# Gated DeltaNet layer: no products with the zero state of a head's first chunk, no update of the state behind its last chunk

## The chip, the cores and the metric

One NeuronCore of a Trainium2 chip runs the whole program. The metric is the device time of one execution in microseconds (us); the kernel before took 1097.52 us in the median of three runs (1096.98 to 1097.6).

## The reference

The sizes are batch 1, 1024 tokens, width 1024 and a depth of one layer, so of the three mixers only the gated DeltaNet runs. It is adaLN modulation (shift, scale and gate from `c`) and RMS norm, one input projection, the mixer, an output projection, a gated residual add and a final RMS norm. The mixer has 8 heads with keys of 128 and values of 256 numbers. Queries, keys and values pass through a causal convolution of four taps and SiLU; queries and keys are normalised. Per head a state S of 128x256 starts at zero, and with a chunk's solved matrices u, w, its attention a and its decayed queries and keys the scan does

```python
def step(S, inp):
    q_c, a_c, u_c, w_c, k_c, gl_c = inp
    v_new = u_c - w_c @ S
    o_c = q_c @ S + a_c @ v_new
    S = S * gl_c + k_c.T @ v_new
    return S, o_c
```

so in the first chunk of a head both products with S are zero, and the S that the last chunk makes is not read. The output is normalised, multiplied by SiLU(z) and projected. All is float32.

## The kernel before

The work is cut into 16 units: unit u = 2*head + par is half `par` (512 tokens) of a head, in 4 chunks of 128 tokens (the kernel's chunks are longer than the reference's; the result is the same). Unit 0 stands ahead of a loop, the loop over `hd` has 7 iterations of two units (an odd one, then an even one), and unit 15 stands behind it. Each engine has its own program, written out by hand, and engines meet by semaphores that only count up; `passed(engine, name, u, n)` waits until maker `name` has counted to n in unit u.

TensorE's program for a unit (`body`) has three kinds of work. One is the input projection of the next unit: six tiles of 24 matmuls each (`project`, L449), a float32 product as three products of high and low parts. It is cut into pieces that stand between the other steps (`fill`; FILLS gives their lengths): by the end of the three merge steps and the piece behind `turn_v` tiles 0, 1 and 2 are done, and tile 3 begins in chunk 0. The second kind is the chunk's matrix inverse (`merge_p`, `merge_d`), and the third the recurrence, per chunk c: K·S (L597), Q·S (L601), a piece of projection, X = inverse · rhs (L609), a piece, the state's increment (L619), the attention's product (L622), a piece, and from chunk 2 on the output projection of chunk c-2 (L567).

Each of these products has a partner elsewhere. VectorE makes the right-hand side `r_rhs` from K·S and the scaled values `vt` (L1232), updates `state` (L1255, after a memset at L1217 in even units) and adds the output's two parts (L1261). ScalarE scales Q·S (`scale_q`, L837) and X (`scale_x`, L843). Semaphores `ks_done`, `qs_done`, `r_done`, `x_done`, `x_out`, `kv_done`, `av_done`, `state_done` and `o_done` count these, four a unit (`state_done` five).

Weight tiles reach TensorE in four steps with two buffers: a DMA of 512 KB issued by SP's queue in a fixed order (`load_tile`, L289), the high part by ScalarE (`split_hi`, L745), the low part by GpSimd (`split_lo`, L1479), the matmuls. The output projection's weights come by the same buffers once per head (`load_wo`, L304), are multiplied by the gate on VectorE (L1111) and split (L751, L1486). For the inverse VectorE makes the matrix of the next unit (`make_n`, L1088), SP takes it through a buffer in HBM into blocks of 16 (L308, L310), VectorE inverts the blocks step by step, SP brings them back (L314, L316), and VectorE spreads them (L1124) for the first merge of the next unit (L513).

Of the kernel before, what the change touches and what calls it, by code (L numbers as in the profile page):

```python
# [7 lines left out]
ALU = mybir.AluOpType  # L8
ACT = mybir.ActivationFunctionType

P = 128
# [4 lines left out]
DV = 256  # L16
# [7 lines left out]
NCH = HALF // P  # L24
# [15 lines left out]
def build(nc, x, c, ada_w, ada_b, norm_w, w_in, conv_w, a_log, dt_bias, gdn_norm_w, w_out,  # L40
          final_norm_w, out):
    ctx = ExitStack()
    with ctx:
# [49 lines left out]
        state = sb("state", [P, DV])  # L93
# [5 lines left out]
        cvk = part(0, 1024, to="p (s t) -> p s t", s=2)  # L99
        cvq = part(1024, 1024, to="p (s t) -> p s t", s=2)  # L100
# [7 lines left out]
        vt = part(5120, 1024, to="p (c t) -> p c t", c=NCH)  # L108
# [324 lines left out]
        def _(pe):  # L433
# [138 lines left out]
            def body(hd, par, last=False, begun=0, fills=FILLS):  # L572
                u = 2 * hd + par
                pos = [begun]
                in_merge, in_v, in_chunk, in_tail = fills

                def fill(n):
                    n = min(n, 2 * MM - pos[0]) if last else n
                    project(u, par, pos[0], pos[0] + n, last)
                    pos[0] += n  # L580

                for lv in range(3):
                    merge_p(u, lv)
                    if lv == 2 and not last:
                        turn_k(u + 1, 1 - par)
                        k_gram(u + 1, 1 - par)
                    fill(in_merge[lv][0])
                    merge_d(u, lv)
                    fill(in_merge[lv][1])
                turn_v(u)  # L590
                fill(in_v)

                for c in range(NCH):
                    passed(pe, "state_done", u, c + 1)
                    if c == 0:
                        passed(pe, "v_scaled", u, 4)
                    nc.tensor.matmul(bank[2][:, 0:DV], cvk[:, par, c * P:(c + 1) * P], state[:, :],  # L597
                                     start=True, stop=True).then_inc(S["ks_done"], 1)
                    passed(pe, "og_done", u, max(c - 1, 0))
                    passed(pe, "qs_scaled", u, c)  # L600
                    nc.tensor.matmul(bank[3][:, 0:DV], cvq[:, par, c * P:(c + 1) * P], state[:, :],  # L601
                                     start=True, stop=True).then_inc(S["qs_done"], 1)
                    if c >= 2:
                        out_project(u, c - 2, 0, hd, par, not last)
                    fill(in_chunk[c][0])
                    if c == 0:
                        passed(pe, "u_merged", u, 3)
                    passed(pe, "r_done", u, c + 1)
                    nc.tensor.matmul(bank[4][:, 0:DV], u_fin[:, c, :], r_rhs, start=True, stop=True  # L609
                                     ).then_inc(S["x_done"], 1)  # L610
                    if c >= 2:
                        out_project(u, c - 2, 1, hd, par, not last)
                    fill(in_chunk[c][1])
                    if c > 0:
                        turn_o(u, c - 1)
                    passed(pe, "x_out", u, c + 1)
                    if c == 0:
                        passed(pe, "kdec_done", u, 1)
                    nc.tensor.matmul(bank[4][:, DV:2 * DV], kdec[:, par, c, :], xs, start=True, stop=True  # L619
                                     ).then_inc(S["kv_done"], 1)  # L620
                    passed(pe, "o_done", u, c)
                    nc.tensor.matmul(bank[5][:, 0:DV], attn_t[:, c, :], xs, start=True, stop=True  # L622
                                     ).then_inc(S["av_done"], 1)
                    fill(in_chunk[c][2])
                fill(in_tail)
                turn_o(u, NCH - 1)
                for n in range(2):
                    out_project(u, NCH - 2, n, hd, par, not last)
                if not last:
                    qk(u + 1, 1 - par)  # L630
                    turn_q(u + 1, 1 - par)
                for n in range(2):
                    out_project(u, NCH - 1, n, hd, par, not last)
# [104 lines left out]
        def _(act):  # L738
# [95 lines left out]
            def scale_q(u, c):  # L834
                passed(act, "qs_done", u, c + 1)
                passed(act, "o_done", u, c)
                nc.scalar.activation(qss, bank[3][:, 0:DV], ACT.Identity, scale=e_gc[:, u, c:c + 1]  # L837
                                     ).then_inc(S["qs_scaled"], 1)
# [24 lines left out]
            def body(hd, par, last=False, first=False):  # L863
# [32 lines left out]
                if not last:  # L896
                    split_hi(u, hd, par, 3)
                for c in range(NCH):
                    scale_q(u, c)
                    if not last:  # L900
                        if c == 0:
                            evacuate_z(u, 2, 1)
                        elif c == 1:
                            evacuate(u, par, hd + par, 3)
                    scale_x(u, par, c)
                    if c > 0:
                        og_high(u, c - 1, last)
# [106 lines left out]
        def _(dve):  # L1014
# [136 lines left out]
            def merge_d_out(u, lv):  # L1151
# [17 lines left out]
                else:  # L1169
                    u_odd = u_fin[0:64, :, 64:P]  # L1170
                    nc.vector.tensor_tensor(u_odd, u_odd, bank[4][0:64, 0:DV].rearrange("p (c w) -> p c w", c=NCH),
                                            ALU.subtract).then_inc(S["u_merged"], 1)

            def norm_y(t):
                if t == 0:
                    dve.wait_ge(fw_in, 16)
                dve.wait_ge(fin_pow, t + 1)
                for j in range(0, D_MODEL, D_MODEL if t < TILES - 1 else HALF):
                    cols = slice(j, D_MODEL if t < TILES - 1 else j + HALF)
                    stt(out=y[:, t, cols], in0=y[:, t, cols], scalar=frs[:, t:t + 1], in1=w_raw[:, 0, cols],  # L1180
                        op0=ALU.mult, op1=ALU.mult).then_inc(fin_done, 1)
# [7 lines left out]
            def body(hd, par, last=False, first=False):  # L1189
# [22 lines left out]
                merge_p_out(u, 2)  # L1212
                if not last:
                    sum_g(u + 1)
                if par == 0:
                    passed(dve, "qs_done", u, 0)
                    nc.vector.memset(state[:, :], 0.0).then_inc(S["state_done"], 1)  # L1217
                else:
                    dve.sem_inc(S["state_done"], 1)
                merge_d_out(u, 2)  # L1220
                if last:
                    silu(u, 0, zt[:, 0, :], gate=True)
# [3 lines left out]
                    make_n(u + 1, other)  # L1226

                for c in range(NCH):
                    passed(dve, "ks_done", u, c + 1)
                    passed(dve, "v_scaled", u, c + 1)  # L1230
                    passed(dve, "x_done", u, c)
                    stt(out=r_rhs, in0=bank[2][:, 0:DV], scalar=neg_egc[:, u, c:c + 1], in1=vt[:, c, :],  # L1232
                        op0=ALU.mult, op1=ALU.add).then_inc(S["r_done"], 1)
                    if c == 0:
                        if last:
                            norm_y(1)
# [13 lines left out]
                            invert_blocks(u + 1, *BASE_STEPS[par][c])  # L1250
                    if c > 0:
                        gate_o(u, c - 1)
                    passed(dve, "kv_done", u, c + 1)
                    passed(dve, "qs_done", u, c + 1)
                    stt(out=state[:, :], in0=state[:, :], scalar=e_gl[:, u, c:c + 1], in1=bank[4][:, DV:2 * DV],  # L1255
                        op0=ALU.mult, op1=ALU.add).then_inc(S["state_done"], 1)
                    passed(dve, "av_done", u, c + 1)
                    passed(dve, "qs_scaled", u, c + 1)
                    passed(dve, "o_turned", u, c - 1)
                    passed(dve, "o_squared", u, c - 1)  # L1260
                    nc.vector.tensor_tensor(o_raw[:, c % 2, :], bank[5][:, 0:DV], qss, ALU.add  # L1261
                                            ).then_inc(S["o_done"], 1)
                    if last and c == 3:
                        gate_o(u, 3)
                    if c >= 2:
# [341 lines left out]
```

## Time and profile before

| | us |
|---|---|
| median of three runs | 1097.52 |
| the profiled execution | 1097.52 |
| its span, first to last instruction | 1095.5 |
| TensorE busy (matmuls) | 1033.7 |
| VectorE busy | 813.2 |
| ScalarE busy | 511.3 |
| GpSimd busy | 498.1 |

An engine's busy time is the time in which at least one of its instructions ran. A float32 product with 256 columns stands in the trace as two matmuls, so 64 products on a line are 128 records. Matmuls overlap: a record's duration is longer than the distance to the next record's start. "Idle before" in square brackets is the time in which the engine did nothing ahead of the instruction, with what ended it. The granted clock is 1.00 at 2.4 GHz and 0.50 at 1.2 GHz.

### The profile page before, as it was taken

To read this page: it belongs to the slowest core of one execution; us is meant where nothing else is said; L and a number is where in the kernel's file an instruction comes from. 1 tells how busy PE (TensorE), PEld (TensorE's weight loads), DVE (VectorE), ACT (ScalarE), POOL (GpSimd) and SP (SyncE) were. 2 spreads that over 40 slices of the span, in tenths; PEclk is the share of its full clock that TensorE was granted. 3 is DMA by queue.
4 is the path that set the end of the run, shared out by engine and by line. 5 is a ranking of instruction groups with operands and counts; after the bars stand their busy time and mean duration, and the time that the engine had idled before them with its cause. 6 is when DMAs were issued, how large, how long until landed. Compare 5 with 4: busy or idle time off the path is not lost.

```text
span 1095.5 us, 20950 instructions
## 1 busy us (share of the span) xinstructions
PE 1033.7 (94%) x6367; PEld 832.0 (76%) x6367; DVE 813.2 (74%) x1757; ACT 511.3 (47%) x1263; POOL 498.1 (45%) x722
## 2 busy tenths in 40 slices
PE   3898699999999999999999999999999999999996
PEld 3766487878778787878878787888878787887864
DVE  4779577697767787597867877686867967687866
ACT  3663444435344543545443543545344453545443
POOL 2242453446444652555435552546435453446424
PEclk9898899999999999999999999999999999999999
DMA  9922222223122221224222231213212241213212
GB/s 316 326 94 79 63 68 64 75 71 88 52 69 70 77 68 51 75 63 107 51 57 59 80 88 51 69 50 102 75 50 59 68 107 51 68 51 86 61 58 115
DMA packets 144440, 91.29 MB, mean 83 GB/s; under 512 B 21526, under 2 KB 136952, under 8 KB 144376
## 3 DMA queue, kind: packets, MB, share of 16 engines
q1 hardware_dynamic: 144376, 90.65, 29.6%
q14 instruction: 50, 0.41, 0.1%
q8 instruction: 14, 0.23, 0.1%
HBM read 81.69 MB, written 8.95 MB: 83 GB/s over the span
## 4 chain that ended last, share of the span: by engine, by line
PE 84%; DVE 5%; issue 5%; ACT 2%; DMA 2%; POOL 2%; SPq 1%; DVEq 0%; POOLq 0%; ACTq 0%
PE bank L449 44%; PE bank L567 17%; PE bank L609 3%; PE bank L597 3%; PE bank L601 2%; PE bank L619 2%; PE bank L622 2%; DVE y L1054 2%; PE bank L647 2%; PE bank L548 1%; PE bank L500 1%; PE bank L474 1%; DMA y<-in_x 1%; PE bank L520 1%; PE bank L539 1%
## 5 line engine op out<-in xcount | busy, mean ns | idle before, releaser
L1479 POOL TENSOR_TENSOR w_lo<-w_raw,w_hi 128x256 fp32r<-128x256 f32 x384 | 309.3, 836 | 277.3 <-ACT w_hi L745 277.3
L449 PE MATMUL bank<-h_hi,w_hi 128*128 128x512 f32 x760 | 328.5, 432 | 6.2 <-ACT w_hi L745 6.2
L449 PE MATMUL bank<-h_lo,w_hi 128*128 128x512 f32 x760 | 299.9, 395 | 0.0
L449 PE MATMUL bank<-h_hi,w_lo 128*128 128x512 f32 x760 | 204.1, 400 | 0.0
L449 PEld LDWEIGHTS bank<-h_hi,w_hi 128*128 128x128 f32 x760 | 143.7, 189 | 38.3 <-ACT w_hi L745 6.9
L1029 DVE SCALAR_TENSOR_TENSOR work<-pre,cw,work 128x512 f32<-128x512 f32 x192 | 160.8, 838 | 12.3 <-ACT work L772 4.2
L449 PEld LDWEIGHTS bank<-h_hi,w_lo 128*128 128x128 f32 x760 | 142.7, 188 | 29.8
L449 PEld LDWEIGHTS bank<-h_lo,w_hi 128*128 128x128 f32 x760 | 144.1, 190 | 26.9 <-issue 0.5
L1521 POOL TENSOR_TENSOR og_lo<-work,og_hi 128x256 fp32r<-128x256 f32 x62 | 45.7, 737 | 211.2 <-ACT og_hi L832 211.2
L567 PE MATMUL bank<-wo_hi,og_hi 128*128 128x512 f32 x248 | 110.1, 444 | 4.1 <-DVE y L1054 4.0
L1054 DVE SCALAR_TENSOR_TENSOR y<-bank,o_rs,y 128x512 f32<-128x512 f32 x128 | 89.8, 743 | 20.9 <-PE bank L567 20.3
L745 ACT ACTIVATE w_hi<-w_raw 128x1024 fp32r<-128x1024 f32 x96 | 101.6, 1058 | 2.1 <-DMA w_raw<-in_gdn_w_in 2.1
L567 PE MATMUL bank<-wo_hi,og_lo 128*128 128x512 f32 x248 | 97.5, 393 | 0.0
L567 PE MATMUL bank<-wo_lo,og_hi 128*128 128x512 f32 x248 | 97.4, 393 | 0.0
L786 ACT ACTIVATE work<-work 128x512 f32<-128x512 f32 x64 | 40.3, 629 | 108.2 <-DVE work L1029 108.2
L1232 DVE SCALAR_TENSOR_TENSOR work<-bank,neg_egc,work 128x256 f32<-128x256 f32 x64 | 30.8, 482 | 78.3 <-PE bank L597 77.5
L1103 DVE TENSOR_TENSOR work<-work 32x15 f32<-32x15 f32 (+7 forms) x240 | 76.8, 320 | 9.7 <-DVE work L1107 1.9
L1036 DVE SCALAR_TENSOR_TENSOR work<-work 128x512 f32<-128x512 f32 x96 | 73.6, 767 | 12.1 <-issue 10.2
L832 ACT ACTIVATE og_hi<-work 128x256 fp32r<-128x256 f32 x62 | 25.9, 418 | 115.8 <-DVE work L1045 107.4
L1486 POOL TENSOR_TENSOR wo_lo<-w_raw,wo_hi 128x256 fp32r<-128x256 f32 x64 | 56.9, 918 | 45.5 <-ACT wo_hi L751 45.5
L1045 DVE SCALAR_TENSOR_TENSOR work<-bank,small,work 128x128 f32<-128x128 f32 x128 | 38.9, 345 | 42.0 <-PE bank L548 41.8
L1107 DVE TENSOR_TENSOR work<-work 32x15 f32<-32x15 f32 (+7 forms) x240 | 62.4, 260 | 8.3
(196 smaller groups left out, 1663.7 us busy)
## 6 DMA issues: line engine op xcount, KB each, us to landing
w_raw<-in_gdn_w_in SPq DMA_DIRECT2D x96, 512.0 KB, 4.0
work<-in_ada_w SPq DMA_DIRECT2D x8, 1024.0 KB, 9.6
w_raw<-in_gdn_w_out SPq DMA_DIRECT2D x16, 512.0 KB, 4.4
y<-in_x SPq DMA_DIRECT2D x8, 512.0 KB, 9.0
work<-in_ada_w SPq DMA_DIRECT2D x8, 512.0 KB, 6.0
n_dram<-work SPq DMA_DIRECT2D x16, 256.0 KB, 2.3
work<-g_dram SPq DMA_DIRECT2D x15, 256.0 KB, 3.9
out<-y SPq DMA_DIRECT2D x7, 512.0 KB, 2.6
```

What stands on the lines that cost most here:

```text
L449: mm = nc.tensor.matmul(bank[m % 2][:, :], w[:, m % 2, k, :], h[:, k, half, :], start=(r == 0), stop=(r == MM - 1))
L567: mm = nc.tensor.matmul(out_bank(c, n, last)[:, :], a[:, m, :], w[:, m, n * 512:(n + 1) * 512], start=(m == 0 and q == 0), stop=(m == 1 an ...
L745: nc.scalar.activation(w_hi[:, k % 2, :, :], w_raw_k[:, k % 2, :, :], ACT.Copy).then_inc(S["w_hi_done"], 1)
L786: nc.scalar.activation(th[:, m % 2, :], cv, ACT.Tanh, scale=0.5).then_inc(S["tanh_done"], 1)
L1029: stt(out=cv, in0=pre[:, r, j:j + HALF], scalar=tap, in1=cv, op0=ALU.mult, op1=ALU.add).then_inc(S["conv_step"], 1)
L1036: stt(out=t, in0=th[:, m % 2, :], scalar=1.0, in1=t, op0=ALU.add, op1=ALU.mult).then_inc(S["silu_done"], 1)
L1054: i = stt(out=yt, in0=out_bank(c, n, last)[:, :], scalar=o_rs[:, c:c + 1], in1=yt, op0=ALU.mult, op1=ALU.add)
L1103: nc.vector.tensor_tensor(tmp, blk_n[:, j:j + 1, j + 1:].rearrange("p o n -> p n o").to_broadcast(shape), blk_y[:, j:j + 1, 0:j + 1].to_br ...
L1107: nc.vector.tensor_tensor(below, below, tmp, ALU.subtract).then_inc(S["base_step"], 1)
L1479: i = nc.gpsimd.tensor_tensor(w_lo[:, k % 2, j:j + 2, :], w_raw_k[:, k % 2, j:j + 2, :], w_hi[:, k % 2, j:j + 2, :].bitcast(F32), ALU.subt ...
L1486: o = nc.gpsimd.tensor_tensor(wo_lo[:, i, j:j + 256], w_raw[:, i, j:j + 256], wo_hi[:, i, j:j + 256].bitcast(F32), ALU.subtract)
L1521: nc.gpsimd.tensor_tensor(gated_lo(c, last), og, gated_hi(c, last).bitcast(F32), ALU.subtract).then_inc(S["og_lo_done"], 1)
```

## The change

TensorE's program: in chunk 0 of an even unit (`fresh`) the products K·S and Q·S go; two semaphore increments stand in their place, behind the same wait for the scaled values, and X takes the scaled values `vt` as its right side in place of `r_rhs`. In chunk 3 of an odd unit the increment of the state goes, with a semaphore increment in its place. ScalarE: the scaling of Q·S in a fresh chunk becomes an increment. VectorE: the memset of the state goes, the right-hand side of a fresh chunk becomes an increment, the state of a fresh chunk is a copy of the product, the last chunk's update becomes an increment, and the output of a fresh chunk is a copy in place of a sum.

```diff
                 for c in range(NCH):
-                    passed(pe, "state_done", u, c + 1)
-                    if c == 0:
+                    fresh = par == 0 and c == 0
+                    if fresh:
                         passed(pe, "v_scaled", u, 4)
-                    nc.tensor.matmul(bank[2][:, 0:DV], cvk[:, par, c * P:(c + 1) * P], state[:, :],
-                                     start=True, stop=True).then_inc(S["ks_done"], 1)
-                    passed(pe, "og_done", u, max(c - 1, 0))
-                    passed(pe, "qs_scaled", u, c)
-                    nc.tensor.matmul(bank[3][:, 0:DV], cvq[:, par, c * P:(c + 1) * P], state[:, :],
-                                     start=True, stop=True).then_inc(S["qs_done"], 1)
+                        pe.sem_inc(S["ks_done"], 1)
+                        pe.sem_inc(S["qs_done"], 1)
+                    else:
...
-                    passed(pe, "r_done", u, c + 1)
-                    nc.tensor.matmul(bank[4][:, 0:DV], u_fin[:, c, :], r_rhs, start=True, stop=True
+                    if not fresh:
+                        passed(pe, "r_done", u, c + 1)
+                    nc.tensor.matmul(bank[4][:, 0:DV], u_fin[:, c, :], vt[:, 0, :] if fresh else r_rhs, start=True, stop=True
                                      ).then_inc(S["x_done"], 1)
...
-                    nc.tensor.matmul(bank[4][:, DV:2 * DV], kdec[:, par, c, :], xs, start=True, stop=True
-                                     ).then_inc(S["kv_done"], 1)
+                    if par == 1 and c == NCH - 1:
+                        pe.sem_inc(S["kv_done"], 1)
+                    else:
...
                 for c in range(NCH):
-                    scale_q(u, c)
+                    if par == 0 and c == 0:
+                        act.sem_inc(S["qs_scaled"], 1)
+                    else:
+                        scale_q(u, c)
...
+            def update_state(u, par, c):
+                passed(dve, "kv_done", u, c + 1)
+                if par == 0 and c == 0:
+                    passed(dve, "qs_done", u, 0)
+                    i = nc.vector.tensor_copy(state[:, :], bank[4][:, DV:2 * DV])
+                else:
+                    passed(dve, "qs_done", u, c + 1)
+                    i = stt(out=state[:, :], in0=state[:, :], scalar=e_gl[:, u, c:c + 1], in1=bank[4][:, DV:2 * DV],
+                            op0=ALU.mult, op1=ALU.add)
+                i.then_inc(S["state_done"], 1)
...
-                if par == 0:
-                    passed(dve, "qs_done", u, 0)
-                    nc.vector.memset(state[:, :], 0.0).then_inc(S["state_done"], 1)
-                else:
-                    dve.sem_inc(S["state_done"], 1)
+                dve.sem_inc(S["state_done"], 1)
...
+                    if par == 0 and c == 0:
+                        dve.sem_inc(S["r_done"], 1)
+                    else:
...
+                    if par == 1 and c == NCH - 1:
+                        dve.sem_inc(S["state_done"], 1)
+                    else:
+                        update_state(u, par, c)
...
+                    if par == 0 and c == 0:
+                        nc.vector.tensor_copy(o_raw[:, c % 2, :], bank[5][:, 0:DV]).then_inc(S["o_done"], 1)
+                    else:
```

## Rows read from the trace of the kernel before

**Rows 1.** The page's busy line: busy us (share of span) and instructions:
```profile
PE 1033.7 (94%) x6367; PEld 832.0 (76%) x6367; DVE 813.2 (74%) x1757; ACT 511.3 (47%) x1263; POOL 498.1 (45%) x722
```

**Rows 2.** Busy by stretch: length, PE, PEld, DVE, ACT, POOL, granted clock, DMA:
```profile
235.00:1040.00 805.00, 795.84 (x4964) 643.52 (x4964) 609.78 (x1354) 374.32 (x948) 390.39 (x549) 1.00 0.27 69
```

**Rows 3.** Timeline of TensorE, unit 4, chunk 0: start us, duration us, line, operation:
```profile
382.57 0.60 PE L597 MATMUL bank<-state,work 128*128 128x256 f32 x2
...
383.25 0.58 PE L449 MATMUL bank<-h_hi,w_hi 128*128 128x512 f32 x1
...
383.66 0.40 PE L449 MATMUL bank<-h_lo,w_hi 128*128 128x512 f32 x1
...
384.13 0.39 PE L449 MATMUL bank<-h_lo,w_hi 128*128 128x512 f32 x1
```

**Rows 4.** Timeline of TensorE, unit 3, chunk 3:
```profile
348.18 0.60 PE L619 MATMUL bank<-work 128*128 128x256 f32 x2
348.62 0.59 PE L622 MATMUL bank<-work 128*128 128x256 f32 x2
```

**Rows 5.** Timeline of ScalarE and TensorE at tile 3, unit 2, then unit 4:
```profile
256.84 1.06 ACT L745 ACTIVATE w_hi<-w_raw 128x1024 fp32r<-128x1024 f32 x1 [0.84 <-DMA w_raw<-in_gdn_w_in]
...
258.29 0.58 PE L449 MATMUL bank<-h_hi,w_hi 128*128 128x512 f32 x1
...
381.06 1.06 ACT L745 ACTIVATE w_hi<-w_raw 128x1024 fp32r<-128x1024 f32 x1 [0.24 <-DMA w_raw<-in_gdn_w_in]
```

**Rows 6.** Timeline of TensorE and ScalarE, unit 0, chunk 0:
```profile
132.49 0.67 PE L597 MATMUL bank<-state,work 128*128 128x256 f32 x2 [1.75 <-ACT work L826]
...
134.47 0.50 PE L449 MATMUL bank<-h_hi,w_hi 128*128 128x512 f32 x1 [0.88 <-ACT w_hi L745]
...
133.36 1.06 ACT L745 ACTIVATE w_hi<-w_raw 128x1024 fp32r<-128x1024 f32 x1 [1.02 <-DMA w_raw<-in_gdn_w_in]
```

**Rows 7.** Timeline of VectorE and TensorE at the ends of units 1 and 3:
```profile
232.32 1.23 DVE L1111 TENSOR_TENSOR w_raw<-w_raw,gate_bc 128x1024 f32<-128x1024 f32 x1 [0.69 <-DMA w_raw<-in_gdn_w_out]
...
234.06 0.68 DVE L1124 TENSOR_TENSOR work<-work,diag_mask 128x512 f32<-128x512 f32 x1
...
234.89 0.44 PE L513 MATMUL bank<-work 128*32 128x16 f32 x32
...
358.50 0.68 DVE L1124 TENSOR_TENSOR work<-work,diag_mask 128x512 f32<-128x512 f32 x1
...
359.89 0.45 PE L513 MATMUL bank<-work 128*32 128x16 f32 x32
```

**Rows 8.** Timeline of GpSimd and TensorE, end of unit 15:
```profile
1080.43 0.73 POOL L1521 TENSOR_TENSOR og_lo<-work,og_hi 128x256 fp32r<-128x256 f32 x1 [4.03 <-ACT og_hi L832]
...
1081.21 0.50 PE L567 MATMUL bank<-wo_hi,og_hi 128*128 128x512 f32 x1
```

**Rows 9.** L212 on TensorE's sequencer: count, duration ns min/median/max, first, last start:
```profile
L212 PEldq EVENT_SEMAPHORE  x15: 51/51/51, 0.9 to 3.0; - x15
```

**Rows 10.** Timeline of VectorE and TensorE, unit 4, chunks 0 and 1:
```profile
388.30 0.48 DVE L1255 SCALAR_TENSOR_TENSOR state<-state,e_gl,bank 128x256 f32<-128x256 f32 x1 [1.25 <-PE bank L619]
...
389.81 0.59 PE L597 MATMUL bank<-state,work 128*128 128x256 f32 x2
```

**Rows 11.** TensorE alone by stretch: stretch, length, busy (records), granted clock, DMA:
```profile
128.76:137.00 8.24, 5.61 (x32) 1.00 0.52 139
...
88.82:92.40 3.58, 0.00 (x2) 0.83 0.38 115
...
91.21:98.04 6.83, 5.64 (x13) 0.50 0.20 49
...
57.08:60.49 3.41, 3.31 (x8) 0.50 0.87 282
```

**Rows 12.** Chain of waits, then timeline of TensorE, at the loop's top:
```profile
298.20 1.73 issue
...
304.79 0.45 PE L517 MATMUL bank<-work 128*32 128x32 f32 x16 [0.65 <-DVE work L1165]
```

More of the change, by code:

```diff
@@ L593, in body @@
                 for c in range(NCH):
-                    passed(pe, "state_done", u, c + 1)
-                    if c == 0:
+                    fresh = par == 0 and c == 0
+                    if fresh:
                         passed(pe, "v_scaled", u, 4)
-                    nc.tensor.matmul(bank[2][:, 0:DV], cvk[:, par, c * P:(c + 1) * P], state[:, :],
-                                     start=True, stop=True).then_inc(S["ks_done"], 1)
-                    passed(pe, "og_done", u, max(c - 1, 0))
-                    passed(pe, "qs_scaled", u, c)
-                    nc.tensor.matmul(bank[3][:, 0:DV], cvq[:, par, c * P:(c + 1) * P], state[:, :],
-                                     start=True, stop=True).then_inc(S["qs_done"], 1)
+                        pe.sem_inc(S["ks_done"], 1)
+                        pe.sem_inc(S["qs_done"], 1)
+                    else:
+                        passed(pe, "state_done", u, c + 1)
+                        if c == 0:
+                            passed(pe, "v_scaled", u, 4)
+                        nc.tensor.matmul(bank[2][:, 0:DV], cvk[:, par, c * P:(c + 1) * P], state[:, :],
+                                         start=True, stop=True).then_inc(S["ks_done"], 1)
+                        passed(pe, "og_done", u, max(c - 1, 0))
+                        passed(pe, "qs_scaled", u, c)
+                        nc.tensor.matmul(bank[3][:, 0:DV], cvq[:, par, c * P:(c + 1) * P], state[:, :],
+                                         start=True, stop=True).then_inc(S["qs_done"], 1)
                     if c >= 2:
@@ L618, in body @@
                         passed(pe, "kdec_done", u, 1)
-                    nc.tensor.matmul(bank[4][:, DV:2 * DV], kdec[:, par, c, :], xs, start=True, stop=True
-                                     ).then_inc(S["kv_done"], 1)
+                    if par == 1 and c == NCH - 1:
+                        pe.sem_inc(S["kv_done"], 1)
+                    else:
+                        nc.tensor.matmul(bank[4][:, DV:2 * DV], kdec[:, par, c, :], xs, start=True, stop=True
+                                         ).then_inc(S["kv_done"], 1)
                     passed(pe, "o_done", u, c)
@@ L1228, in body @@
                 for c in range(NCH):
[L1229 to L1233, printed above, removed]
+                    if par == 0 and c == 0:
+                        dve.sem_inc(S["r_done"], 1)
+                    else:
+                        passed(dve, "ks_done", u, c + 1)
+                        passed(dve, "v_scaled", u, c + 1)
+                        passed(dve, "x_done", u, c)
+                        stt(out=r_rhs, in0=bank[2][:, 0:DV], scalar=neg_egc[:, u, c:c + 1], in1=vt[:, c, :],
+                            op0=ALU.mult, op1=ALU.add).then_inc(S["r_done"], 1)
                     if c == 0:
@@ L1252, in body @@
                         gate_o(u, c - 1)
[L1253 to L1256, printed above, removed]
+                    if par == 1 and c == NCH - 1:
+                        dve.sem_inc(S["state_done"], 1)
+                    else:
+                        update_state(u, par, c)
                     passed(dve, "av_done", u, c + 1)
@@ L1260, in body @@
                     passed(dve, "o_squared", u, c - 1)
-                    nc.vector.tensor_tensor(o_raw[:, c % 2, :], bank[5][:, 0:DV], qss, ALU.add
-                                            ).then_inc(S["o_done"], 1)
+                    if par == 0 and c == 0:
+                        nc.vector.tensor_copy(o_raw[:, c % 2, :], bank[5][:, 0:DV]).then_inc(S["o_done"], 1)
+                    else:
+                        nc.vector.tensor_tensor(o_raw[:, c % 2, :], bank[5][:, 0:DV], qss, ALU.add
+                                                ).then_inc(S["o_done"], 1)
                     if last and c == 3:
```

## The prediction

> **What bounds the kernel now.** I first read the busy line of the page. TensorE is busy 1033.7 us of the span, 94% [rows 1]. Then I asked for one long stretch of the loop over heads, from 235 to 1040 us: TensorE is busy 795.84 of 805.00 us, 99%, at the full granted clock, with VectorE at 609.78 [rows 2]. So in the loop TensorE has 9.2 us without work, and an instruction taken from it shortens the loop, as long as nobody it waits for has become the last one. The question is therefore twofold: what one of the removed products takes of TensorE's stream, and at which of the places the stream can't close up because a tile, a DMA or another engine arrives only then.
>
> I call a head's first half unit 2*head and its second half unit 2*head+1. Each of the 8 heads loses two products (L597, L601) in chunk 0 of its even unit and one (L619) in chunk 3 of its odd unit, 24 of the 256 products on L597, L601, L619 and L622.
>
> **What a product takes.** In unit 4 the first state product starts at 382.57 and the second projection matmul behind the pair at 383.66, 1.09 us later; the projection matmuls of the tile follow each other in 0.23 us (two distances from 383.66 to 384.13) [rows 3]. Without the pair the first projection matmul stands where the first product stood, and the second comes 0.23 us later. So a pair is worth 1.09 - 0.23 = 0.86 us, 0.43 a product. The product behind the last chunk agrees: it starts at 348.18 and the next at 348.62 [rows 4], 0.43 to 0.44 us. If all 24 closed up it would be 24 x 0.43 = 10.3 us. Now place by place.
>
> **Pairs of units 4 to 14.** What is late next is the weight tile behind the pair (tile 3), split by ScalarE on L745. In unit 4 that split starts at 381.06 and takes 1.06, so it ends at 382.12; its first matmul starts at 383.25 [rows 3, 5]: 1.13 us in hand. The matmul of head 0 that does wait for such a split starts 0.05 us after it (133.36 + 1.06 = 134.42, then 134.47) [rows 6], so 1.08 us can be taken out and 0.86 is. I take unit 4 for all six (units 4, 6, 8, 10, 12, 14): 6 x 0.86 = 5.2 us.
>
> **Pair of unit 2.** Here the same split waited 0.84 us for its DMA, ends at 256.84 + 1.06 = 257.90, and the matmul starts at 258.29 [rows 5]. Only 0.39 - 0.05 = 0.34 us can go, and the remaining 0.52 becomes a wait for ScalarE.
>
> **Pair of unit 0.** TensorE sat idle 1.75 us before the pair, and then again 0.88 us until a tile 3 whose split waited 1.02 us for a DMA [rows 6]. Nothing removed here brings that DMA forward: 0 us. The same place has a price, below.
>
> **Products behind the last chunk.** In units 3, 5, 7, 9, 11 and 13 the stream goes on with the next product and with projections. The DVE chain at the unit's end (add y, gate the output weights, attention, spread) starts from TensorE's own results and moves with it. The merge that opens the next unit (L513) starts at 359.89, the spread it waits for ends at 358.50 + 0.68 = 359.18 [rows 7], 0.71 us earlier: covered for 0.43. If the DMA of the output weights landed only just in time there, these six would give nothing; I see no wait for it in unit 3 and take 6 x 0.43 = 2.6 us. In unit 1 there is such a wait: the gating on L1111 sat idle 0.69 us for that DMA, the spread ends at 234.06 + 0.68 = 234.74, and L513 starts at 234.89 [rows 7]. 0.15 - 0.05 = 0.10 us can go. In unit 15 the matmul of 1081.21 starts just behind GpSimd's split of 1080.43 + 0.73 = 1081.16 [rows 8], and that chain comes from a transpose ahead of the removed product: 0 us.
>
> Sum of what closes up: 5.2 + 0.34 + 2.6 + 0.10 = 8.2 us.
>
> **The rest of the edit.** 24 increments replace the products on TensorE. The 15 increments of the start take 51 ns each on its sequencer [rows 9]; the queue ahead of them hides that (0.05 x 24 = 1.2 us if it didn't, all in a row). I take 0. A copy of the state replaces memset and the fused update: the update of unit 4 took 0.48 us, ended at 388.78, and the next state product starts at 389.81 [rows 10], so it has 1.03 us in hand; a copy that is slower by that much would still cost nothing. VectorE no longer waits for the first state product and can make the next unit's matrix earlier, so its DMAs through n_dram start earlier, on a queue (SP's) that then comes to the next weight tile earlier; nobody on the path waits for them today: 0. On ScalarE one scaling per head goes, beside the idle time that the projections cover: 0.
>
> **The price in head 0.** With the pair gone TensorE does nothing from 132.49 - 1.75 = 130.74 to 134.47 us [rows 6], 3.73 us in one piece instead of 1.75 and 0.88. Before, it kept the full clock across these two gaps (1.00 over 128.76 to 137.00). An idle stretch of 3.58 us earlier (88.82 to 92.40) shows 0.83 as the granted clock, so it fell inside it, and the next 6.83 us ran at 0.50 with TensorE busy 5.64 of them; another half-clock stretch, 57.08 to 60.49, held 3.31 us of work [rows 11]. At half the clock (1.2 of 2.4 GHz) half of that time is lost: 1.7 us by the short one, 2.8 us by the long one. The new gap is 0.15 us longer than the one that brought the long one, but which of the two follows depends on when in the gap the clock falls, so I take the middle, 2.2 us; both ends stay in the range, and below them 0 for no fall. The Trainium skill (TensorE: Matmul & The Clock Gate, "Why this matters for your kernels") says that idle gaps between bursts of matmuls bring the lower clock back; by that rule the fall comes, and the case without one, below, would go.
>
> **Sum.** The profiled execution took 1097.52 us for a span of 1095.5, 2.0 around it, and is the median itself. 8.2 - 2.2 = 6.0 us off gives 1091.5 us.
>
> **Rivals.**
> *The clock doesn't fall in head 0.* Then the whole 8.2 us stay: 1089.3. For it: the two gaps now there were taken without a fall [rows 6, 11]. Against it: the 3.58 us gap.
> *The wait takes the product's place in all heads.* If the tile 3 of every even unit comes as late as in unit 2, the seven pairs give 7 x 0.34 = 2.4 instead of 5.5 us, and with 2.7 for the last chunks and the clock's 2.2 it comes to 1094.6. For it: two of the first three even units show a split that waits for its DMA. Against it: in unit 4 1.08 us are in hand.
> *An increment drains TensorE.* If it waited for the matmuls before it, each of the 14 places would cost about the difference between a matmul's duration and its distance to the next, 0.40 - 0.23 = 0.17 [rows 3], and a weight load, 832.0 us for 6367 of them or 0.13 [rows 1]: 14 x 0.30 = 4.2 us, which leaves 1095.7, no change that can be told. For it: the increments of before ran while the engine had nothing to do [rows 9]. Against it: the sequencer's waits stand before every tile and every state product, and the stream does not open there [rows 3].
> *The loop's top, on the other side.* At the top of the loop's second iteration the chain of waits runs through 1.73 us of issue time between two instructions of VectorE, and TensorE then waits 0.65 us on L517 for VectorE's transpose; the loop has seven iterations [rows 12]. VectorE's program gets another length ahead of the loop and inside it. If that puts one more such stop ahead of the transpose, each iteration loses 1.73, 7 x 1.73 = 12.1 us, and the time is 1103.6. It decides from 6.0 / 7 = 0.86 us an iteration on. For it: the stops are there, and nothing else explains them. Against it: few instructions change, so a stop may as well fall away.
>
> **Chances.** The forecast 0.55; no fall 0.2; the wait in all heads 0.1; the drain 0.07; the loop's top 0.05; the remaining 0.03 for something else that takes the gain. The predicted time is 1091.5. The range takes in no fall (1089.3), with some 1 us less at the loop's top, and the wait in all heads (1094.6): 1088.0 to 1095.0. What a measurement can tell from no change is 0.2%, 2.2 us, so "faster" is below 1095.3: the first three and part of the last, 0.87; "same" is the drain and a little of the rest, 0.08; slower 0.05.
>
> **What would show it.** L597 and L601 should have 56 products each instead of 64, L619 also 56, and TensorE's busy time in the loop should fall by about as much as the span. From unit 4 on, an even unit's first tile-3 matmul should follow the last matmul of tile 2 in 0.23 us. In unit 2 that matmul should wait about 0.5 us for L745. In head 0 TensorE should show one gap of some 3.7 us and a granted clock of half behind it. The L513 of unit 2 should wait for the spread. I am wrong if TensorE shows new idle time behind the increments, if the matmuls of other even units wait for L745, if the waits at the loop's top grow, or if the clock stays up in head 0.

## The result, and the profile after

The changed kernel took 1088.07 us (median of 4 runs, 1087.1 to 1089.54) against 1097.56 us for the kernel before beside it: ratio 0.9905, 95% interval 0.9888 to 0.9922. So 0.95% came off, some 9.5 to 10.4 us, where 6.0 was forecast; the time lies at or just below the low end of the forecast's range. The span of the profiled execution went from 1095.5 to 1086.9 us, 8.6 less; the sums below go by these spans (the profiled execution of after, 1088.6 us, is 0.5 slower than its median). (One run of an experiment, of the kernel with a filled gap and 8 increments, took 1702.8 us at a clock of 0.56; it is in none of the ratios below.)

Page of after, busy line, which answers to [rows 1]:

```profile
PE 1024.2 (94%) x6319; PEld 824.1 (76%) x6319; DVE 801.7 (74%) x1733; ACT 507.8 (47%) x1255; POOL 499.7 (46%) x722
```

TensorE has 48 records fewer (two for a product) and lost 9.5 us of work. To see the loop alone I take busy time by stretch from the L513 of unit 2 to the L513 of unit 15 (columns as in [rows 2]); after, then before:

```profile
237.71:1037.03 799.32, 792.54 (x4953) 640.19 (x4953) 604.06 (x1340) 375.15 (x955) 393.46 (x550) 1.00 0.27 70
```
```profile
234.89:1045.66 810.77, 801.34 (x4993) 647.82 (x4993) 613.74 (x1360) 378.54 (x962) 391.12 (x550) 1.00 0.26 69
```

The stretch is 11.45 us shorter, and TensorE's busy time in it fell by only 8.80: idle time went from 9.43 to 6.78. The removed products explain the first number, something else gave 2.65 us more, and 11.45 is more than the span lost because head 0, ahead of the loop, became longer. To place this, I cut the timelines of TensorE at two marks that every unit has, the start of its merge (L513, the first of unit u) and its first and last product with the inverse (X, L609 before, L616 after), and sum over units. Microseconds:

| kernel | even units 2 to 14: L513 to X of chunk 0 | odd units 3 to 13: L513 to X of chunk 0 | odd units 1 to 13: X of chunk 3 to next L513 | start of unit 1's L513 | span |
|---|---|---|---|---|---|
| before | 177.84 | 159.31 | 99.71 | 172.81 | 1095.5 |
| after | 171.46 | 156.70 | 96.91 | 175.85 | 1086.9 |
| e1: 1 increment | 171.50 | 158.33 | 96.54 | 174.15 | 1086.4 |
| e2: gap filled | 171.44 | 156.38 | 96.49 | 174.27 | 1084.5 |
| e3: pairs alone | 171.46 | 156.36 | 99.50 | 172.39 | 1085.6 |
| e4: last chunks alone | 177.83 | 158.86 | 96.85 | 173.64 | 1093.0 |
| e5: before, 31 increments | 177.81 | 154.23 | 99.69 | 174.96 | 1094.2 |
| e6: filled, 4 increments | 171.44 | 160.08 | 96.56 | 174.62 | 1088.6 |
| e7: filled, 8 | 171.44 | 154.50 | 96.53 | 174.14 | 1082.5 |
| e8: filled, 12 | 171.44 | 154.62 | 96.52 | 174.26 | 1083.3 |
| e9: 8 increments | 171.50 | 154.76 | 96.64 | 174.96 | 1083.7 |
| e10: after once more | 171.53 | 156.62 | 96.72 | 177.61 | 1088.3 |
| e11: e7 once more | 171.47 | 154.24 | 96.49 | 173.19 | 1081.3 |

The first column holds the removed pairs (unit 0 lies in the fourth), the second the loop's top in its six later iterations, the third the products behind a last chunk, the fourth head 0. After against before: -6.4, -2.6, -2.8, +3.0, together -8.7, and the span says -8.6. No odd unit lost a product in front of its first X, so the 2.6 us of the second column are the part that the forecast did not have.

Timeline of TensorE and ScalarE after, against [rows 3 to 5 and 7]: unit 2's L513 and its tile 3, the end of unit 3, tile 3 of unit 4:

```profile
237.71 0.45 PE L513 MATMUL bank<-work 128*32 128x16 f32 x32 [0.33 <-DVE work L1137]
...
258.66 1.10 ACT L755 ACTIVATE w_hi<-w_raw 128x1024 fp32r<-128x1024 f32 x1
...
260.43 0.39 PE L449 MATMUL bank<-h_hi,w_hi 128*128 128x512 f32 x1
...
349.42 0.60 PE L632 MATMUL bank<-work 128*128 128x256 f32 x2
349.67 0.58 PE L449 MATMUL bank<-h_hi,w_hi 128*128 128x512 f32 x1
...
381.56 1.98 PE L449 MATMUL bank<-h_hi,w_lo 128*128 128x512 f32 x8
383.37 0.39 PE L449 MATMUL bank<-h_hi,w_hi 128*128 128x512 f32 x1
383.60 0.39 PE L449 MATMUL bank<-h_lo,w_hi 128*128 128x512 f32 x1
```

In unit 4 the stream runs through the place of the pair in steps of 0.23 us with no gap: the increments there do not drain the engine. In unit 2 the split of tile 3 waits for nothing and ends at 258.66 + 1.10 = 259.76, 0.67 us ahead of its matmul.

Head 0, in the timeline of TensorE and by stretch (all engines), against [rows 6, 11]:

```profile
134.69 0.80 PE L449 MATMUL bank<-h_hi,w_hi 128*128 128x512 f32 x1 [4.46 <-ACT w_hi L755]
```
```profile
131.00:134.69 3.69, 0.00 (x0) 0.00 (x0) 1.76 (x8) 2.13 (x5) 0.00 (x0) 0.91 1.07 289
134.00:140.83 6.83, 6.14 (x14) 4.81 (x15) 0.00 (x0) 3.03 (x5) 2.79 (x4) 0.50 0.56 140
```

One idle piece of 4.46 us, where 3.73 was foretold, and from 134.00 on 6.83 us at half the clock (1.2 GHz), with 6.14 us of work in them. From that matmul to the L513 of unit 1 it is 41.16 us, against 38.34 before (134.47 [rows 6] to 172.81): the half clock costs 2.82 us. The other 0.22 of the 3.0 us is tile 3 itself, which starts later.

The loop's top, timeline of VectorE at the loop's second iteration, before and after:

```profile
300.06 0.42 DVE L1148 TENSOR_TENSOR pm<-bank,pair_mask 128x256 f32<-128x256 f32 x1 [1.86 <-issue]
300.40 0.16 DVE L1186 TENSOR_SCALAR q_eps<-q_ss 128x4 f32<-128x4 f32 x1
302.30 0.69 DVE L1036 SCALAR_TENSOR_TENSOR work<-work 128x512 f32<-128x512 f32 x1 [1.74 <-issue]
302.91 0.75 DVE L1029 SCALAR_TENSOR_TENSOR work<-pre,cw,work 128x512 f32<-128x512 f32 x1
```
```profile
301.76 0.43 DVE L1161 TENSOR_TENSOR pm<-bank,pair_mask 128x256 f32<-128x256 f32 x1 [1.65 <-issue]
302.10 0.20 DVE L1210 TENSOR_SCALAR q_eps<-q_ss 128x4 f32<-128x4 f32 x1
302.22 0.68 DVE L1049 SCALAR_TENSOR_TENSOR work<-work 128x512 f32<-128x512 f32 x1
304.19 0.75 DVE L1042 SCALAR_TENSOR_TENSOR work<-pre,cw,work 128x512 f32<-128x512 f32 x1 [1.29 <-issue]
```

VectorE stops twice in an iteration without waiting for any engine. Before, the second stop stood ahead of the SiLU product (L1036); after, that product (L1049) runs and the stop stands one instruction later, ahead of the convolution (L1042). The work of both is the same. The waits (total us, times, longest us) add it up over six iterations (the loop's first iteration has neither stop), before and then after:

```profile
DVE pm L1148 <- issue: 10.5, 6, 1.9
DVE work L1036 <- issue: 10.2, 6, 1.8
...
PE bank L517 <- DVE work L1165: 4.8, 8, 0.7
```
```profile
DVE pm L1161 <- issue: 10.0, 6, 1.9
DVE work L1042 <- issue: 8.1, 6, 1.5
...
PE bank L517 <- DVE work L1178: 2.7, 8, 0.8
```

The second stop costs 2.1 us less, and TensorE waits 2.1 us less for the transpose behind it. Two theories for that. A: the stop belongs to a position in VectorE's program; the change takes one instruction net from what VectorE runs ahead of the loop (312 records before, 311 after, waits and increments among them, register operations left out), so the same position falls one instruction later in the loop. B: VectorE simply has less to do (no fused update behind a last chunk, a copy for another). Beside these stands C, for head 0: the half clock comes from the idle piece that the pair left.

### The profile page after: what moved, and what is told of

Read it like the earlier page. It is cut to its first block, busy times and chain, and to the rows that moved or that the text cites. A ratio compares the mean times of both kernels' runs of the same rounds, so it can differ in the third digit from the quotient of the medians.

```text
span 1086.9 us, 20802 instructions
## 1 busy us (share of the span) xinstructions
PE 1024.2 (94%) x6319; PEld 824.1 (76%) x6319; DVE 801.7 (74%) x1733; ACT 507.8 (47%) x1255; POOL 499.7 (46%) x722
## 4 chain that ended last, share of the span: by engine, by line
PE 81%; DVE 7%; issue 4%; DMA 3%; ACT 2%; POOL 2%; SPq 1%; DVEq 0%; POOLq 0%; ACTq 0%
PE bank L449 43%; PE bank L567 16%; PE bank L616 3%; PE bank L632 2%; PE bank L603 2%; PE bank L607 2%; PE bank L629 2%; DVE y L1067 2%; PE bank L657 2%; PE bank L548 1%; PE bank L500 1%; PE bank L474 1%; DVE work L1042 1%; DMA w_raw<-in_gdn_w_out 1%; DMA y<-in_x 1%
## 5 line engine op out<-in xcount | busy, mean ns | idle before, releaser
L1505 POOL TENSOR_TENSOR w_lo<-w_raw,w_hi 128x256 fp32r<-128x256 f32 x384 | 305.4, 826 | 270.0 <-ACT w_hi L755 270.0
L1042 DVE SCALAR_TENSOR_TENSOR work<-pre,cw,work 128x512 f32<-128x512 f32 x192 | 161.0, 839 | 19.6 <-issue 8.1
L1049 DVE SCALAR_TENSOR_TENSOR work<-work 128x512 f32<-128x512 f32 x96 | 71.4, 744 | 13.9 <-ACT work L791 12.2
L853 ACT ACTIVATE work<-bank,k_tab 128x256 f32<-128x256 f32 x64 | 30.3, 474 | 76.3 <-PE bank L616 76.3
```

Source lines behind the costliest of these rows:

```text
L1042: stt(out=cv, in0=pre[:, r, j:j + HALF], scalar=tap, in1=cv, op0=ALU.mult, op1=ALU.add).then_inc(S["conv_step"], 1)
L1049: stt(out=t, in0=th[:, m % 2, :], scalar=1.0, in1=t, op0=ALU.add, op1=ALU.mult).then_inc(S["silu_done"], 1)
L1505: i = nc.gpsimd.tensor_tensor(w_lo[:, k % 2, j:j + 2, :], w_raw_k[:, k % 2, j:j + 2, :], w_hi[:, k % 2, j:j + 2, :].bitcast(F32), ALU.subt ...
```

## Experiments

**First set: e1 to e4**, beside the kernel before (median 1096.7 us of 13 runs).

e1 gives the missing position back: one increment of a semaphore that nobody waits for, on VectorE ahead of head 0.

```diff
+        pad = sem("pad")
...
+            for _ in range(1):
+                dve.sem_inc(pad, 1)
             body(0, 0, first=True)
```

> The changed kernel with one more semaphore increment in VectorE's program, on a semaphore nobody waits for, just ahead of unit 0. Theory A (the stop at the loop's top is tied to a position in VectorE's program, and the edit made that program one instruction shorter ahead of the loop): the stop comes one instruction earlier again, ahead of the SiLU of the unit's start instead of behind it, TensorE's waits for L517 and L532 go back from 4.4 us in all to about 7, and the span grows by 2 to 3 us against the changed kernel. Rival B (VectorE simply has less to do since the change): one increment of 21 ns changes nothing, the waits stay at 4.4 us and the span within 0.5 us, apart from the clock in head 0.

Its waits:

```profile
DVE work L1050 <- issue: 9.9, 6, 1.8
DVE pm L1162 <- issue: 9.6, 6, 1.7
...
PE bank L518 <- DVE work L1179: 4.8, 8, 0.8
```

L1050 is the SiLU product: the stop is back ahead of it, TensorE's wait is the 4.8 us of before, and the loop's top lost 1.6 of its 2.6 us, with every product still removed. That is A. The 1.0 us that stay are not the second stop's. Most of them go with the first: TensorE's wait on L532 behind it is 2.1 us in all before, 1.7 in after and 1.3 in e1, as that stop takes 10.5, 10.0 and 9.6; why it varies is open. The time does not show the loss: 1088.8 us, ratio 0.9928 (0.9912 to 0.9945), an interval that overlaps the changed kernel's, and instead of the 2 to 3 us more that were expected the span is even 0.5 below after's, since in this execution the half clock behind the gap lasted 3.41 us and unit 1 started 1.7 us earlier.

e2 fills the gap of head 0 with nine products into a bank that is free there and whose content nobody reads:

```diff
+                    if isinstance(u, int) and u == 0 and c == 0:
+                        passed(pe, "evacuated", u, 2)
+                        for _ in range(9):
+                            nc.tensor.matmul(bank[1][:, 0:DV], ident[:, :], cvk[:, 0, 0:DV], start=True, stop=True)
                     if fresh:
                         passed(pe, "v_scaled", u, 4)
```

> The changed kernel with nine products without use (identity times keys, into a bank that is free) on TensorE in chunk 0 of unit 0, where it sits idle 4.46 us; their result is not read. Theory C (the clock falls in that gap and costs 3.1 us of the span): the granted clock stays at 1.00 from 128 us on, tile 3 of unit 0 starts when its split is done as before, and the span is 2 to 3.5 us shorter than that of the changed kernel, 1083.5 to 1085. Rival (the loss in head 0 is made good later, where units 1 and 2 wait for DMAs): the clock stays up, but the span moves by less than 1 us.

Busy time by stretch of e2, then of after (TensorE alone):

```profile
131.00:134.50 3.50, 3.50 (x22) 3.12 (x21) 2.16 (x9) 2.20 (x6) 0.77 (x1) 1.00 0.82 217
134.50:143.00 8.50, 8.50 (x39) 6.90 (x38) 1.90 (x3) 3.97 (x7) 5.78 (x8) 1.00 0.53 132
```
```profile
131.00:134.50 3.50, 0.00 (x0) 0.93 1.06 288
134.50:143.00 8.50, 8.31 (x24) 0.63 0.38 95
```

39 matmuls in the second stretch instead of 24: the clock stays at 2.4 GHz, and C holds. What the fall costs can be read in all thirteen profiles, from the first matmul of tile 3 to the L513 of unit 1: 38.3 to 38.4 us in the eight without a fall there (before, e2 to e4, e6 to e8, e11), 39.7 to 39.9 in the three with 3.41 us at half the clock (e1, e5, e9), 41.1 to 41.2 in the two with 6.83 (after, e10). The time of e2, 1085.2 us, ratio 0.9893 (0.9877 to 0.991), can't be told from the changed kernel's ratio; e9 and e11 below stand side by side.

e3 keeps the pairs removed and puts the last chunk's product and the fused update back:

```diff
-                    if par == 1 and c == NCH - 1:
-                        pe.sem_inc(S["kv_done"], 1)
-                    else:
+                    if True:
...
-                    if par == 1 and c == NCH - 1:
-                        dve.sem_inc(S["state_done"], 1)
-                    else:
-                        update_state(u, par, c)
+                    update_state(u, par, c)
```

> Only the pairs of the first chunks go; the product and the update behind the last chunk stay as in the kernel before. Theory A: seven pairs give 0.9 us each, 6.4 us, the loop's top gives its 2 to 3 us, since VectorE's program ahead of the loop has the changed kernel's length, and the clock in head 0 takes 1.7 to 3.1 us back: 5.5 to 7 us off the kernel before. Rival B (less work on VectorE): the loop's top gives nothing or half, as the odd units' last update, the one that stands near the loop's top, is still there: 3 to 5 us off.

1089.94 us, ratio 0.9946 (0.9929 to 0.9964). The third column is back to 99.50, the first and the second stand as after. So the loop's top has its full gain although VectorE does the last chunk's update again: that is against B. The median fell by 6.8 us, as expected, but the span by 9.9, because in this execution the clock did not fall behind the gap (unit 1 at 172.39). The gap was shorter here; the timelines of TensorE give 3.48 us in e3 (no half clock behind it), 3.81 in e1 and 4.21 in e9 (3.41 us of half clock), 4.46 in after and 4.56 in e10 (6.83 us).

e4 is the other half: products and work of the pairs as before, only the last chunk's product removed.

```diff
-                    fresh = par == 0 and c == 0
+                    fresh = False
...
-                if par == 0 and c == 0:
-                    passed(dve, "qs_done", u, 0)
-                    i = nc.vector.tensor_copy(state[:, :], bank[4][:, DV:2 * DV])
-                else:
+                if True:
...
+                if par == 0:
+                    passed(dve, "qs_done", u, 0)
+                    nc.vector.memset(state[:, :], 0.0).then_inc(S["state_done"], 1)
```

> Only the product and the update behind the last chunk go; first chunks are as in the kernel before, with memset. Theory A: six units give 0.43 us and unit 1 about 0.25, 2.8 us in all; the loop's top stays as before (waits for L517 and L532 of about 7 us), since VectorE's program ahead of the loop has the old length, and the clock stays up in head 0: 2.5 to 3 us off. Rival B: the odd units' update is gone, so the loop's top shortens too: 4.5 to 5.5 us off.

1095.34 us, ratio 0.9988 (0.9973 to 1.0003), which by itself can't be told from no change. The span is 2.5 us shorter: 2.9 us off in the third column, 0.45 at the loop's top, and unit 1 starts 0.8 later. The fused update is gone here and the wait is still there (waits of TensorE in e4):

```profile
PE bank L517 <- DVE work L1175: 5.1, 8, 0.8
```

So B falls: the update can stay (e3) or go (e4), and the stop keeps to the length of the program ahead of it.

**Second set: e5 to e8** (before: 1098.2 us, 10 runs). If the stop belongs to a position, it can be moved without any change to the work. e5 is the kernel before with 31 increments on VectorE ahead of the loop:

```diff
+        pad = sem("pad")
...
+            for _ in range(31):
+                dve.sem_inc(pad, 1)
             dve.wait_ge(g_stored, 16)
             spread_t(0)
```

> The kernel before, with all 24 products, and 31 semaphore increments on a semaphore nobody waits for in VectorE's program ahead of unit 0, where VectorE waits for a DMA anyway. If programs are fetched in blocks of 8, 16 or 32 instructions, 31 more is the same place in a block as one fewer, the changed kernel's. Theory A: the stop at the loop's top comes one instruction later, behind the SiLU, TensorE's waits for L517 fall from 4.8 to about 2.5 us and the span by 2 to 2.6 us with no product gone (1094.9 to 1095.5). Rival B (the loop's top gains only because VectorE has less to do): waits and time stay as before.

1094.11 us, ratio 0.9968 (0.9956 to 0.9979): faster, with all 24 products in place. Its waits:

```profile
DVE pm L1149 <- issue: 9.7, 6, 1.7
DVE work L1233 <- issue: 2.4, 7, 0.4
...
PE bank L518 <- DVE work L1166: 1.0, 2, 0.8
```

The second stop left the loop's top (-5.1 us in the second column). A shorter one, of some 0.3 us, turned up among the chunks; there, between the first and the last X of the odd units, 1.6 us came back. (e3 has a short one too, 1.9 us over seven times on L1056.) What these short ones wait for is not shown.

e6, e7 and e8 take the changed kernel with e2's gap filled and put 4, 8 and 12 such increments at e5's place (the diffs of e2 and e5 with these counts).

> The kernel with nine products in head 0's gap, and 4 more increments in VectorE's program ahead of unit 0. Theory A: the stop moves by four instructions, ahead of the reads that L1161's successor needs or, if that wraps round a block, to four fewer than a block later; with blocks of 8 it lands behind the first transpose of the unit, and L517's waits fall under 1 us (1.5 to 2 us off the version without the increments); with blocks of 16 or more it stands earlier and L517's waits are 5 us or more (2 us on). Rival B: no change.

> The same with 8 increments. Theory A: with blocks of 8 the same as none (L517's waits about 2.4 us, 1085 us); with blocks of 16 the stop lands eight instructions later, behind the transpose: L517's waits under 1 us and 1083 to 1084 us. Rival B: no change in either.

> The same with 12 increments. Theory A: with blocks of 8 as with 4; with blocks of 16 the stop lands four instructions later than with none, near the first convolution: L517's waits between 0.5 and 2 us, 1083.5 to 1085 us. Rival B: no change.

e6: 1090.29 us, 0.9927 (0.9908 to 0.9946); e7: 1084.17 us, 0.9872 (0.9848 to 0.9895); e8: 1084.63 us, 0.9872 (0.9851 to 0.9892). With four increments the stop went further up, two recorded instructions ahead of where after has it, to L1215, the second of the loop, and TensorE waits 6.1 us:

```profile
DVE q_eps L1215 <- issue: 11.4, 6, 2.0
DVE pm L1166 <- issue: 10.0, 6, 1.8
...
PE bank L518 <- DVE work L1183: 6.1, 8, 0.9
```

With 8 and 12 it is gone and only the first stop stays. The position holds, the lengths of a piece that the expectations tried do not: with 8 instructions, e7 would have the stop where e2 has it, with 16 it would stand later in e7 and e8, with 32 e5 would have it where after has it.

**Third set: e9 to e11** (before: 1096.92 us, 7 runs). e9 is the changed kernel with 8 increments, e10 the changed kernel once more, e11 the kernel of e7 once more, with gap filled and 8 increments.

> The changed kernel with 8 more increments in VectorE's program ahead of unit 0, and without the products in head 0's gap. Theory A: the second stop at the loop's top is gone, L517's waits fall from 2.7 to about 1 us and the loop's top gives another 2 us against the changed kernel; the clock in head 0 falls in some executions and not in others, at 1.7 to 3.1 us: 1085 to 1088 us. Rival B: as the changed kernel, 1087 to 1089.5.

> The changed kernel once more, beside the two others. Theory C (the fall in head 0 comes at most executions, but its length depends on when in the gap it comes): 1087 to 1089.5 us, and the profile shows a half-clock stretch of 3.4 or 6.8 us behind the gap; unit 2's pair again gives the whole 0.9 us. Rival (the fall in the first profile was an exception): no half-clock stretch behind the gap, and 3 us less in the profiled execution, near 1084 us of span.

> The changed kernel with both, nine products in head 0's gap and 8 increments: 1083.5 to 1085 us, 2 to 4 us under the changed kernel of the same call, the clock at 1.00 in head 0's chunk 0 and no second stop at the loop's top. If the two effects overlapped it would be no faster than the version with increments alone.

e9: 1085.59 us, 0.9895 (0.9879 to 0.9912). e10: 1087.16 us, 0.9902 (0.9886 to 0.9919). e11: 1083.65 us, 0.988 (0.9863 to 0.9897): 3.5 us below the changed kernel beside it and 13.3 below the kernel before, the best of all. In the two profiled executions the half clock makes 1.5 us of the difference between e9 and e11; three of the four runs of e11 lie below all of e9's. Waits of e11, and then, of the pages of after and of e11, the line of one of the two instruction queues (packets, MB, share):

```profile
DVE pm L1166 <- issue: 9.8, 6, 1.7
...
PE bank L518 <- DVE work L1183: 1.0, 2, 0.8
```
```profile
q14 instruction: 50, 0.41, 0.1%
```
```profile
q14 instruction: 44, 0.36, 0.1%
```

Six packets fewer, in a loop in which the second stop occurred six times. The kernels whose loop's top has the second stop (before, after, e1 to e4, e6, e10) all show 50 packets, those without it 44 (e7, e9, e11) or 45 (e5, e8). In stretches of 0.25 us, the profile of after has one such packet at 299.75 to 300.00 and one at 302.25 to 302.50; VectorE stops at 300.11 and at 302.90 and goes on at 301.76 and 304.19, each time 1.7 to 2.0 us after the packet. In e11 the packets lie at 296.69 to 296.94, with the stop, and at 299.08 to 299.33, without one; what e11 lacks is the next packet, which after has at 305.50 to 305.75. I read the two stops as VectorE waiting for its program: ahead of the first instruction of the loop (L1161 in after), and again where the piece fetched for it ends. What the runs show is the position, the packets and their times; what a packet holds they don't show.

The Trainium skill (Runtime: NRT & Kernel Launch, "Instruction fetch mechanics") says that a taken branch to a target outside the two pages held forces a fetch before execution goes on. The trace agrees with it in the first stop, 1.65 us in after, which the loop's first iteration, reached without that branch, does not have. The same section calls the cost of passing from one block to the next mostly hidden; if the second stop is such a passage, just behind the branch it was not, 1.29 us in after and 1.74 before, and the measurement decides.

## Why the prediction was right in direction and short in size

**What bounds the kernel**: right. TensorE stayed the bound, and a product taken from its stream shortened the loop where nothing else was late.

**Pairs of units 4 to 14**: right, 0.91 us each instead of 0.86, 5.5 instead of 5.2 us.

**Pair of unit 2**: wrong, 0.90 instead of 0.34 us. The step failed at its premise, that without the pair the DMA of tile 3 still comes as late as with it [rows 5]. The split waits for that DMA in the other two profiles with the pair as well, e4 and then e5:

```profile
257.50 1.06 ACT L755 ACTIVATE w_hi<-w_raw 128x1024 fp32r<-128x1024 f32 x1 [1.04 <-DMA w_raw<-in_gdn_w_in]
```
```profile
259.34 1.06 ACT L746 ACTIVATE w_hi<-w_raw 128x1024 fp32r<-128x1024 f32 x1 [0.98 <-DMA w_raw<-in_gdn_w_in]
```

In the ten without it that wait is nothing (0.26 us in e2). The DMA is issued 16.9 to 17.1 us behind unit 2's L513 in all thirteen; it lands 5.0 to 5.2 us later in the three with the pair and 3.8 to 4.1 in the others. Only in those three does a packet of 16 KB of the other instruction queue, 0.92 to 0.99 us long, lie in the middle of the transfer (at 254.09 us before). I take it for the cause, which no run tests; why it lies elsewhere without the pair is open. The rival that put this wait into all heads had nothing for it. (It counted two of the first three even units as waiting for this DMA; by [rows 5, 6] it is all three, unit 4 with 0.24 us and time in hand.)

**Pair of unit 0**: right that nothing closes up; its first matmul of tile 3 starts at 134.69 instead of 134.47.

**Products behind the last chunk**: right, 2.8 us instead of 2.7. Unit 1 gave 0.25 instead of 0.10, and the L513 behind it does wait for the spread, 0.33 us, as foretold. Unit 15 gave nothing: from its L513 to the end it is 49.84 us before and 49.85 after.

**The increments**: right at 0. Each of the three lines has the foretold 56 products, two records each; two of them, by line:

```profile
L603 PE MATMUL bank<-state,work x112: 377/377/483, 144.0 to 1066.4; 128*128 128x256 f32 x112
L629 PE MATMUL bank<-work x112: 377/379/483, 141.8 to 1065.1; 128*128 128x256 f32 x112
```

**The clock in head 0**: the mechanism right, the size short, 3.0 us against the 2.2 taken. The long stretch came, and its price of 2.82 us is the bound of 2.8 that the prediction gave it; the short one cost 1.4 to 1.6, against 1.7. The other 0.22 us is tile 3, which started later. The gap was longer than worked out because its two ends move by themselves: the first matmul of tile 3 waits for a split that waits for a DMA, and the earlier end, 130.23 instead of 130.74 us, follows the clock of the prologue, at half from 121.93 to 128.76 us before and from 123.77 to 127.18 in after. That the length of the half clock behind the gap depends on when it falls, as the prediction has it, is borne out: it begins 0.69 and 0.79 us ahead of the gap's end in after and e10 (long), 0.09 ahead in e9 and 0.95 behind it in e1 (short). What I could not read from one execution is how much this varies. The start of unit 1 lies between 172.39 and 177.61 in the thirteen profiles, the rival without a fall was one of them (e3), and a fall of 3.41 us came in e5 as well, with the pair in place between two gaps of 1.75 us.

**The loop's top**: this is the step that failed, 0 in the sum and 2.6 us on the chip, 2.1 of them in TensorE's wait behind the second stop. I saw the stop and TensorE's wait behind it [rows 12], and treated it as a danger with one sign: another stop, at 5%, with a gain there left to some 1 us of the range. I wrote that VectorE's program gets another length ahead of the loop, and did not go on to ask where the stop that is already there would slide to; the 0.65 us that TensorE waits behind it in an iteration was the gain that lay ready (in six iterations, not in the seven of the rival's sum). e1, e4, e5 and e6 show that it goes by position and not by work.

Where the forecast had 6.0, the measured terms are 6.4 + 2.8 + 2.6 - 3.0 = 8.8, against 8.6 of span. Two errors of size (unit 2 and head 0, +0.56 and -0.84) nearly cancel, which is luck, and the loop's top is nearly all of the rest. What stays open: how long a piece of program is, and what puts the half clock of the prologue at other places from execution to execution.

## What to carry to other kernels

An "issue" stop at a loop's top that follows a position in the program and not an engine is part of the sum: count the instructions that a change adds or removes ahead of it, and try a few increments without effect: eight were worth 1.9 us at the loop's top of the changed kernel (e9 against e10; 1.6 between the medians, whose runs overlap), 31 were worth 0.32% in the kernel before (e5), and four made it worse, by 3.7 us at the loop's top (e6 against e2). Work removed from the bounding engine at a place where it waits anyway can cost its clock; filling the gap with products that nobody reads was worth 1.9 us (e11 against e9). A wait for a DMA seen in the kernel before need not stay when the program changes: unit 2's was there in all three profiles with the pair and gone, or nearly, in the ten without it.

## What the runs showed of the hardware that was not expected

VectorE's two stops at the loop's top come with single packets of an instruction queue of about 8 KB (0.41 MB in 50 packets), and VectorE goes on 1.7 to 2.0 us after one. The price of the second stop depends on the place: 8.1 us over six iterations ahead of the convolution, 10.2 one recorded instruction earlier, 11.4 two earlier, none with eight increments. A packet of the other instruction queue in the middle of a weight tile's transfer went with a landing about 1 us later, in three profiles of three. And the half clock behind head 0's gap, which differs between kernels whose work there is the same, went from nothing to 6.83 us over gaps of 3.48 to 4.56 us.
